# Hybrid decoder layer on one core: x comes transposed from the host, 1/rms is applied where the projections leave PSUM, and the final norm takes one root for both tiles of rows

## What is computed

```python
h = rms_norm(x, g_mix)                 # x * rsqrt(mean(x*x) + eps) * g_mix
proj = h @ w_in + b_in                 # 1024 -> 6416 columns
gq, gk, gv, gr, g_lr, sq, sk, sv, gate_a, gate_b = split(proj)
...                                    # gated linear attention (gq, gk, gv, gr, g_lr)
...                                    # sliding-window attention with sinks (sq, sk, sv)
mixed = sigmoid(gate_a) * y_a + sigmoid(gate_b) * y_b
x = x + mixed @ w_out
x = x + moe_ffn(rms_norm(x, g_ffn), ...)   # top 4 of 32 experts, all float32
return rms_norm(x, g_final)
```

## Time and profile before

| | |
|---|---|
| median of 3 runs | 1194.38 us (1194.31 to 1195.21) |
| profiled execution, its own time | 1193.74 us |
| its span, first to last instruction | 1191.9 us |
| PE busy | 1139.2 us (96%), 7389 products |
| DVE / ACT / POOL busy | 423.3 / 256.7 / 141.8 us |
| HBM read | 446.12 MB |
| mean granted TensorE clock | 0.997 of full |

### The profile page before, as it was taken

How to read it: one execution, slowest core, us unless ns; L and a number is a source line. 1 busy time by engine, 2 the same in 40 slices (tenths; PEclk the granted TensorE clock), 3 DMA queues, 4 the chain that set the end, 5 groups by cost and what they waited for, 6 DMA issues and landing times.

```text
span 1191.9 us, 17974 instructions
## 1 busy us (share of the span) xinstructions
PE 1139.2 (96%) x7389; PEld 553.3 (46%) x7389; DVE 423.3 (36%) x817; ACT 256.7 (22%) x442; POOL 141.8 (12%) x103
## 2 busy tenths in 40 slices
PE   7999999999999999999999999999999999999996
PEld 5988999984333333333333333333333333333332
DVE  6988744854222222222222222222222222222223
ACT  5465746332111111111111111111111111111112
POOL 5545543561000000000000000000000000000000
PEclk9999999999999999999999999999999999999999
DMA  7634336789999999999999999999999999999995
GB/s 283 248 145 158 111 138 251 292 317 368 426 427 428 428 427 433 429 433 429 434 434 429 434 428 435 429 433 429 433 431 432 431 432 432 432 426 427 430 427 233
DMA packets 27331, 447.68 MB, mean 376 GB/s; under 512 B 3216, under 2 KB 3344, under 8 KB 5632
## 3 DMA queue, kind: packets, MB, share of 16 engines
q1 hardware_dynamic: 26640, 446.05, 89.2%
q0 software_dynamic: 224, 0.71, 0.2%
q10 hardware_dynamic: 432, 0.42, 0.1%
HBM read 446.12 MB, written 1.05 MB: 375 GB/s over the span
## 4 chain that ended last, share of the span: by engine, by line
PE 55%; DMA 37%; DVE 6%; issue 1%; ACT 1%; DVEq 0%; SPq 0%
DMA ring<-wexp 36%; PE PS L896 31%; PE PS L623 12%; PE PS L889 3%; PE PS L881 2%; PE PS L913 1%; PE PS L672 1%; PE PS L748 1%; DMA EXT<-be 1%; DVE slot_R L1269 1%; PE PS L722 1%; DVE EXT L1307 1%; DVE SQ L1721 0%; DVE SQ L1724 0%; PE PS L735 0%
## 5 line engine op out<-in xcount | busy, mean ns | idle before, releaser
L896 PE MATMUL PS<-ring,SQ 128*64 128x512 f32 x1536 | 350.1, 597 | 20.5 <-DMA ring<-wexp 19.2
L896 PE MATMUL PS<-ring,PTG 128*64 128x512 f32 x1024 | 240.2, 600 | 10.3 <-DMA ring<-wexp 10.2
L896 PEld LDWEIGHTS PS<-ring,SQ 128*64 128x64 f32 x1536 | 103.7, 136 | 233.2 <-issue 199.0
L1216 ACT ACTIVATE SQ<-SQ 128x256 f32<-128x256 f32 x64 | 26.7, 417 | 600.0 <-DVE SQ L1717 600.0
L547 POOL TENSOR_TENSOR slot_R<-ring,slot_R 128x512 fp32r<-128x512 f32 (+1 forms) x76 | 117.8, 1581 | 99.9 <-ACT slot_R L1013 99.9
L896 PEld LDWEIGHTS PS<-ring,PTG 128*64 128x64 f32 x1024 | 66.5, 136 | 132.2 <-issue 129.9
L896 PE MATMUL PS<-EXT,SQ 128*64 128x512 f32 x512 | 116.9, 598 | 0.9 <-DMA EXT<-wexp 0.2
L1717 DVE TENSOR_SCALAR SQ<-PS 128x256 f32<-128x256 f32 x64 | 27.2, 425 | 243.2 <-PE PS L896 243.2
L623 PE MATMUL PS<-slot_R 128*128 128x256 f32 (+2 forms) x288 | 90.1, 313 | 0.0
L1013 ACT ACTIVATE slot_R<-ring 128x2048 fp32r<-128x2048 f32 (+1 forms) x38 | 70.8, 1869 | 39.1 <-DMA ring<-wblk 22.0
L889 PE MATMUL PS<-PTG,BRW 64*128 64x512 f32 x264 | 74.2, 640 | 0.8 <-DVE PTG L1736 0.8
(11 more groups left out here) (277 smaller groups left out, 1143.4 us busy)
## 6 DMA issues: line engine op xcount, KB each, us to landing
ring<-wexp SPq DMA_DIRECT2D x50, 4096.0 KB, 30.1
ring<-wexp SPq DMA_DIRECT2D x59, 2048.0 KB, 19.2
EXT<-wexp SPq DMA_DIRECT2D x10, 4096.0 KB, 39.6
ring<-wblk SPq DMA_DIRECT2D x36, 1024.0 KB, 4.8
EXT<-wexp SPq DMA_DIRECT2D x12, 2048.0 KB, 20.5
ring<-wexp SPq DMA_DIRECT2D x2, 1024.0 KB, 33.4
BRW<-brow SPq DMA_DIRECT2D x7, 256.0 KB, 6.0
ring<-wskv SPq DMA_DIRECT2D x2, 544.0 KB, 9.3
```

The lines of the kernel that those rows point to most:

```text
L896: last = mm(PS[g * SLOTS:(g + 1) * SLOTS, b, :], lhsT, rhs[:, g * 512:(g + 1) * 512], start=start, stop=stop)
L1216: fn(SGM[:, part], GLU[:, part], ACT.Sigmoid, scale=ALPHA).then_inc(sgm_ready, 1)
```

## The change

1. The host also hands over x transposed (`xt`). ScalarE rounds xt times g_mix straight from it (`high_x`), VectorE takes the remainder (`low_x`). The transposes on TensorE go. Unit 0 and 1 are split in halves (`first_split`, `first_rest`, Pool takes the other halves of the remainders), and `first_block` orders its products by pieces of x.
2. x itself is loaded behind unit 2. Squares, variance and root follow on ScalarE and VectorE behind unit 2's split; the product that spreads 1/rms over the partitions stands in block 1 (`scales_across`), and its copy to RSR (now in a place of its own) behind use 3.
3. Token-major evacuations multiply by 1/rms per partition and add the bias. Feature-major uses are evacuated by VectorE (`feature_major` there, product with RSR), and ScalarE then adds bias and function in SBUF.
4. The order of a few loads changes with it, and chunk 1 waits for use 25, since RSR lies in its slot.
5. Final norm: all four squares first, one sum, variance, root and reciprocal for both tiles; ScalarE then scales tile 0 and stores it, VectorE tile 1, stored by SyncE.

```diff
@@ SyncE
+                if u == 0:
+                    x_columns(0)
+                    half = unit_width(0) // 2
+                    sp.dma_start(w_unit(0)[:, 0:half], wblk[0, :, 0:half]).then_inc(unit_in[w_slot(0)], 16)
+                    sp.dma_start(w_unit(0)[:, half:2 * half], wblk[0, :, half:2 * half]).then_inc(first_in, 16)
+                    x_columns(1)
...
+                if u == 2:
+                    for i in range(TT):
+                        sp.dma_start(X[:, i, :], x[i * P:(i + 1) * P, :]).then_inc((x_in, x_in1)[i], 16)
+                    bias(0)
+                if u == 3:
+                    bias(1)
+                    sp.dma_start(TAB[:, T_SWA:NTAB], tab[:, T_SWA:NTAB]).then_inc(tab_in, 16)
@@ ScalarE
+            for u in range(2):
+                high_x(2 * u)
+                first_split(u, 0)
+                high_x(2 * u + 1)
+                first_split(u, 1)
+            split(2)
             for i in range(TT):
                 act.wait_ge((x_in, x_in1)[i], 16)
                 fn(SQ[:, i, :], X[:, i, :], ACT.Square, accum_out=S_SS[:, i:i + 1]).then_inc(ssq0, 1)
             act.wait_ge(var0, 1)
             fn(S_SD, S_VAR, ACT.Sqrt).then_inc(sd0, 1)
...
             def feature_major(i, dst, c, func):
                 for half in range(2):
-                    u = 2 * i + half
-                    act.wait_ge(pj_full[u % NPJ], u // NPJ + 1)
+                    evacuated(act, 2 * i + half)
                     for f in range(2):
-                        n = 2 * half + f
-                        last = fn(dst[half][:, f * SEQ:(f + 1) * SEQ], PS[:, u % NPJ, f * SEQ:(f + 1) * SEQ], func,
-                                  bias=col(c + n))
-                    last.then_inc(pj_free[u % NPJ], 1)
+                        part = dst[half][:, f * SEQ:(f + 1) * SEQ]
+                        last = fn(part, part, func, bias=col(c + 2 * half + f))
+                    last.then_inc(gates_done, 1)
@@ TensorE
-            dense(1)
+            dense(1, {(0, 1): [scales_across]})
@@ VectorE
-                last = v.tensor_tensor(dst, bk(u % NPJ, w), BRW[:, n % 2, 0:w], ALU.add)
+                rs = S_RS[:, u % 2:u % 2 + 1]
+                last = v.scalar_tensor_tensor(dst, bk(u % NPJ, w), rs, BRW[:, n % 2, 0:w], ALU.mult, ALU.add)
...
+            def feature_major(u, dst):
+                dve.wait_ge(pj_full[u % NPJ], u // NPJ + 1)
+                v.tensor_tensor(dst.rearrange("p (f t) -> p f t", f=2), bk(u % NPJ).rearrange("p (f t) -> p f t", f=2),
+                                RSR.unsqueeze(1).broadcast_to([P, 2, SEQ]), ALU.mult).then_inc(pj_free[u % NPJ], 1)
...
                 if u == 3:
+                    dve.wait_ge(rsr_full, 1)
+                    link(v.tensor_copy(RSR, PS[:, 3, 0:SEQ]))
                     rotate_queries(0)
@@ ScalarE, end
+            for i in range(TT):
                 act.wait_ge(moe_done, i + 1)
                 for n in range(2):
                     fn(OUTB[:, i, n * BW:(n + 1) * BW], bk(2 * i + n), ACT.Square,
                        accum_out=S_SQ[:, 2 * i + n:2 * i + n + 1]).then_inc(ssqf, 1)
...
+            act.wait_ge(varf, 1)
+            fn(S_SD, S_VAR, ACT.Sqrt).then_inc(sdf, 1)
+            act.wait_ge(rsf, 1)
+            for n in range(2):
+                half = slice(n * BW, (n + 1) * BW)
+                act.wait_ge(xg_ready, n + 1)
+                fn(OUTB[:, 0, half], XG[:, 0, half], ACT.Copy, scale=S_RS[:, 0:1]).then_inc(out_a, 1)
```

More of the change, by code:

```diff
@@ L509, in _ @@
             sp.dma_start(GF, gfin.partition_broadcast(P)).then_inc(gfin_in, 16)
[L510 to L515, removed]
+            for n in range(2):
+                half = slice(n * BW, (n + 1) * BW)
+                sp.wait_ge(out_ready, n + 1)
+                sp.dma_start(out[P:2 * P, half], OUTB[:, 1, half]).then_inc(out_done, 16)
             sp.wait_ge(out_done, 2 * 16 * TT)
@@ L577, in _ @@
             mm = nc.tensor.matmul
[L580 to L593, removed]
             usage = [0]
@@ L658, in first_block, with product @@
                 banks = [pj_bank(), pj_bank()]
[L659 to L664, removed]
-                    w = (h_unit(u, True), w_unit(u, True))[b]
[L666 to L676, removed]
+                def product(u, a, b, k):
+                    w = (h_unit(u, True), w_unit(u, True))[b]
+                    for half in range(2):
+                        last = mm(bk(banks[half]), HT2[a][:, KH * u + k, half * P:(half + 1) * P],
+                                  w[:, k * BW:(k + 1) * BW], start=(u + a + b + k == 0),
+                                  stop=(u == 1 and b == 1 and k == KH - 1), skip_group_check=True)
+                        if b == 1 and k == KH - 1 and (u or half):
+                            last.then_inc(pj_full[banks[half]] if u else first_used, 1)
@@ L1225, in _ @@
             preload(ACT.Sqrt)
-            def squares(i):
+            for i in range(TT):
                 act.wait_ge(moe_done, i + 1)
@@ L1403, in decay_products @@
                 if level == 0:
-                    for u in range(6, 10):
-                        evacuated(dve, u)
+                    dve.wait_ge(gates_done, 4)
                     dve.wait_ge(decay_out, 1)
@@ L1429, in _ @@
             v.scalar_tensor_tensor(W0, TMP, -1.0, TMP, ALU.mult, ALU.min).then_inc(gate_neg, 1)
+            for half in range(2):
+                feature_major(6 + half, GQT[:, half * BW:(half + 1) * BW])
             rest(10)
@@ L1437, in _ @@
                 v.tensor_copy(qT[:, 2 * a:2 * a + 2, :], PS[:, 4 + a, :].rearrange("p (k t) -> p k t", k=2)).then_inc(qt_ready, 1)
+            for half in range(2):
+                feature_major(8 + half, GKT[:, half * BW:(half + 1) * BW])
             mask = TAB[:, T_SWA:T_SWA + SEQ]
@@ L1528, in rest_t @@
                                     ALU.subtract).then_inc(done, 1)
+            dve.wait_ge(gr_ready, 3)
+            for half in range(2):
+                feature_major(18 + half, MIX[half])
             rest_t(OB2, obt_full, obt_lo)
             rest(24)
+            for half in range(2):
+                feature_major(20 + half, MIX[2 + half])
             dve.wait_ge(gla_zero, 1)
```

187 lines of the change are left out of this document (107 added, 80 removed).

## The result

The changed kernel takes 1205.36 us (median of 4 runs, 1203.81 to 1205.72), the kernel before 1194.8 us beside it on the same chip (1194.31 to 1196.08): a ratio of 1.0092 with a 95% interval of 1.0075 to 1.0108, **slower by about 11 us**. The forecast, 1202.1 us, had the sign and the places of the waits right and 3 us too little.

The account below looks back on a forecast made before the run. TensorE ahead of the first used-chunk load (284.38 us) was taken as the bound, the expert loop following at fixed distance. Terms summed to +7.7 us: 1201.4 us profiled, 1202.1 us forecast median; 1195.5 to 1205.5 us, 8 in 10.

Parts of the forecast that it names:

- First product near 7.6 us: Kernel start: TensorE's first products begin near 7.6 us, where they began at 11.86 us before.
- Start, -1.1 us: Block 1: products come 4.3 us forward, but bank 0 waits behind unit 3's remainder on VectorE; -1.1 us, between -3.9 and 0.
- Row of scales, +0.4 us: The 256-wide copy of the scales enters VectorE's unbroken chain ahead of the rotation; +0.4 us, 0 to 0.5.
- Use 8 free at 78.0 us: Keys: VectorE frees use 8 only after the gate chain and query copies, delaying TensorE's use 11; +3.5 us, 2.5 to 4.5.
- Use 6, free at 60.75 us: Gate inputs: VectorE evacuates use 6 behind the gate's first step, TensorE wants the bank at 58.8 us; +2.0 us, 1.6 to 2.4.
- The rival that I gave 0.17: After the 3.5 us wait ahead of use 11 TensorE's clock falls, adding 1.7 us: 1203.8 us; chance 0.17.
- Attention, +0.5 us: Attention: Pool's next split starts later against VectorE because ScalarE's key biases precede it; +0.5 us, 0 to 1.5.
- Use 18, wait of 2.4 us: Output gates: VectorE frees use 18 behind a remainder, at 154.2 us; use 21 wants its bank at 151.85 us; +2.4 us.
- Use 24, +0.6 us: End of attention output: VectorE's late remainder makes TensorE wait 1.2 us, 0.6 us replacing an existing wait; +0.6 us, 0 to 1.6.
- Tail, -0.6 us: Final norm: the last store goes out at 1188.5 us instead of 1189.07 us; -0.6 us, -0.8 to +0.3.
- never last: Every bank comes free before TensorE asks, so the whole head start stays: -4.5 us, 1189.9 us; chance 0.13.
- VectorE undisturbed: VectorE's rotations run at 0.69 us, use 6 is free in time, use 8 about 0.7 us late: 1196.4 us; chance 0.10.

Follow-up runs that it names:

- experiment 6: Changed kernel with ScalarE issuing the load of TAB ahead of that of CV, as the kernel before does: 1205.36 us, ratio 1.0087.
- experiment 10: Changed kernel, VectorE's scalings moved, old final norm, unit 13's split before key biases, use 8 behind the decay scan, mean square before unit 2's remainder: 1194.3 us, 1.0004.
- experiment 1: Changed kernel plus 7, 15 and 9 filler products on TensorE before its waits for uses 6, 8 and 18: 1206.3 us, ratio 1.0102.
- experiments 8 and 9: Changed kernel with VectorE's scalings and unit 3's remainder moved, old final norm: 1196.28 us; the same with ScalarE's split of unit 13 before the key biases: 1194.84 us.
- keys_early: Changed kernel with VectorE's scaling of use 8 ahead of the decay sums instead of behind the query copies: 1203.94 us, ratio 1.0087.
- tab_first: Changed kernel with TAB's load issued ahead of CV's on ScalarE (the same run as experiment 6): 1205.36 us, ratio 1.0087.
- queries_early: Changed kernel with VectorE's evacuations of uses 6 and 7 ahead of and between the keys' rotations: 1204.7 us, ratio 1.0086.
- all_moved: Changed kernel with unit 3's remainder and the scalings of uses 6, 7, 8, 18 and 19 placed elsewhere on VectorE, old final norm: 1196.28 us, ratio 1.0022.

## Why the prediction was right and wrong, point by point

- **What bounds the kernel: right.** The loss was made ahead of the first used-chunk load and reached the end nearly whole (12.56 us there, 11.9 us in the span). I had no term for the loop taking back 0.8 us.
- **First product near 7.6 us: wrong, 9.30 us.** I took x's half for the last to come. ScalarE's first operation needs TAB, which took 5.62 us to land where it took 3.98 us before, and experiment 6 shows that the order of the two small tables doesn't matter: whichever goes second is late.
- **Start, -1.1 us: wrong, 0.** The mechanism was the named one (bank 0 behind the remainder of unit 3, a wait of 1.46 us), but that remainder began at 23.42 us, not at 21.8 us. I had unit 3's split at 19.9 us, by its load; in the changed kernel ScalarE began it at 21.5 us, behind the root, for which it had stood 2.56 us. In experiment 10, where the root is early, the load holds it to 21.82 us, 1.9 us later than I took it. How long before 21.5 us the unit had landed in the changed kernel is not shown.
- **Row of scales, +0.4 us: +0.2 us, by luck.** TensorE goes on behind use 5 at 44.59 us, 44.43 us before. The copy takes 0.41 us as priced, but a rotation step behind it ran at 0.69 us where it took 1.82 us before; in experiment 6 it took 1.80 us and TensorE went on at 45.66 us.
- **The first step that failed in the sum:** I added the start's -1.1 us to terms that were worked out from absolute times of VectorE's chain. The times at which TensorE would want the banks, 58.8 and 74.5 us, leave that gain out, and the sum puts it in. Use 8 free at 78.0 us against 72.1 us before is +5.9 us, whatever TensorE won earlier; my terms up to there make only +4.8 us. Measured: 77.88 us, +5.8 us. **The absolute time was right to 0.1 us, its conversion into terms was not**, though so close a hit is partly luck: in experiment 6, nearly the same program, TensorE goes on at 78.96 us. A gain ahead of a wait for a chain that does not depend on it is no term at all.
- **Use 6, free at 60.75 us: 60.4 us measured. Use 18, wait of 2.4 us: 2.3 us.** Both right.
- **The second step that failed, and the larger: the sum puts the clock at nothing.** The rival that I gave 0.17 came true on top of the forecast, and twice where it counted. I had put it only behind the longest wait and at 1.7 us; there it cost 1.8 us at the scores. It also came behind the shorter waits of 1.8 and 2.3 us. This is the largest part of what I missed, 3.6 us in the trace. The Trainium skill (TensorE: Matmul & The Clock Gate, Part 1: The HAM clock gate) has the array fall to 1.2 GHz after idling; the trace agrees in kind. The dip of the earlier trace rows is no case of it, as I had read it: TensorE was busy for all of the first 15.00 us there. What experiment 1 adds is that the dips' price and their worth differ: with all of them gone the load came back by only 1.5 us and was still 11.0 us late, where my terms up to there make 8.3 us. So the clock alone does not account for the miss: with the clock full, 1.4 us were lost in the attention, where I had 0.5 us.
- **Token-major evacuations at nothing: slightly wrong.** The multiply-add takes 0.74 us for 512 columns where the addition took 0.69 us, 0.48 against 0.42 us for 256 and 0.23 against 0.17 us for 16; over the eight up to use 5 that is 0.4 us, of which 0.3 us fall from use 2 on, where VectorE works without a pause.
- **Attention, +0.5 us: 0 in the changed kernel,** I take it because TensorE came so late that VectorE had caught up; in experiment 1, where it came 1.2 us earlier, the attention lost 1.4 us. The collision that I named for it is real and shows when TensorE is early (experiments 8 and 9).
- **Use 24, +0.6 us: 0.85 us,** of that mechanism: the new wait is 0.92 us where I had 1.2 us, but it replaces only 0.3 us of the old one and not 0.6 us. **Tail, -0.6 us: +0.1 us.** I priced the issue of the last store and not what the DMA engines still had to move.

The sum as it should have stood: 5.8 to use 11, 1.8 clock, 0 attention, 2.3 use 18, 1.8 clock, 0.85 use 24 = 12.55 us at the load; -0.8 loop, +0.1 tail = 11.9 us. The rival "never last" needs no wait for VectorE's evacuations; there are four. "VectorE undisturbed" needs rotations at 0.69 us and use 6 free in time: seven of the twelve steps over 512 columns took 1.6 to 1.8 us, and TensorE waited 1.8 us for use 6.

## What to carry to other kernels

When work moves from an engine with slack to one whose queue has long stretches without a pause, don't price the work, price its place: here 0.6 us pieces, alone or in pairs, cost 2 to 4 us where they stood behind work that could wait, and 8 of 11 us came back by moving them and one remainder alone. Work out when each buffer comes free in absolute time and subtract what the consumer wanted before; never add a head start to such a difference. And look once at what the moved wait now holds up on its own engine: here the key biases held a split on ScalarE, that shifted Pool, and Pool slowed VectorE.

## What the runs showed of the hardware that I had not expected

The length of a wait does not settle whether the clock falls. Chains of keys_early, tab_first, queries_early and the changed kernel at the same place, behind waits of 2.4, 2.1, 2.3 and 2.3 us:

```profile
158.84 3.13 PE PS L620 x24
```

```profile
163.43 3.13 PE PS L620 x24
```

```profile
159.78 4.62 PE PS L620 x24
```

```profile
161.75 4.28 PE PS L620 x24
```

The same 24 products take 3.13 us at full clock in two kernels and 4.3 to 4.6 us with a dip in the other two. The Trainium skill (TensorE: Matmul & The Clock Gate, Part 1: The HAM clock gate) has the number of slow products at a kernel's start vary from run to run. In these four it varies whether a dip comes at all. Over the traces of all the kernels here up to 300 us, leaving out the first product of each: none of the waits of 0.8 to 1.64 us was followed by a dip, of the eight of 1.77 to 2.36 us five were, and all four of 3.6 to 4.0 us were. The dip at the router comes with no wait of over 0.3 us before it. The dips cost 1.5 to 1.8 us each, and once, behind 3.6 us (tab_first, use 8), 2.7 us (twelve products of 512 columns in 5.49 us, from 78.96 us). So near 2 us a wait should be priced as the wait, plus 1.5 to 1.8 us with even chances or a little more.

Pool's split draws out some of VectorE's operations and not others: additions and products with both operands in SBUF go from 0.60 to 1.70 us apiece from start to start, while evacuations from PSUM keep their 0.74 us beside it (in all_moved the one at 84.13 us, inside Pool's 78.51 to 85.37 us). Two operands are not needed: the copy of one bf16 operand among the bias steps (L1334, 217.51 us) went from 0.69 to 1.67 us.
